# A TensorE gate step in fp32r halves, with GpSimd making the low half, and exponentials placed behind the gate steps

## What is computed

```python
def peer_ffn(h, peer_wq, peer_k1, peer_k2, peer_u, peer_v):      # 512 tokens, 8 heads, 128 x 128 keys
    s1, s2 = ...                                     # scores of each head's two query halves with 128 keys
    v1, i1 = lax.top_k(s1, 16)
    v2, i2 = lax.top_k(s2, 16)
    cand = (v1[..., :, None] + v2[..., None, :]).reshape(T, PEER_HEADS, 256)
    sc, pos = lax.top_k(cand, 16)
    e1 = jnp.take_along_axis(i1, pos // 16, axis=-1)
    e2 = jnp.take_along_axis(i2, pos % 16, axis=-1)
    experts = e1 * 128 + e2                                      # 8 x 16 = 128 experts a token
    gates = jax.nn.softmax(sc, axis=-1)
    ...
    a = gelu(einsum("ckd,cd->ck", peer_u[experts], h)) * gates
    return einsum("ck,ckd->cd", a, peer_v[experts])
```

## Time and profile before

| | |
|---|---|
| median of 3 runs | 2980.7 us (2978.4 to 2987.61) |
| the profiled execution | 2978.2 us |
| its span | 2976.5 us |
| TensorE busy | 2824.8 us, 95% |
| VectorE busy | 2235.7 us, 75% |
| ScalarE busy | 1481.7 us, 50% |
| GpSimd busy | 582.0 us, 20% |
| up stage | about 1784 to 2428 us |
| down stage | from 2431 us |

### The profile page before, as it was taken

One profiled execution on the slowest core, in us unless ns is written; L12 is line 12 of the kernel. 1 busy time (PEld: TensorE's weight loads), 2 busy tenths in 40 slices (PEclk: granted clock), 3 DMA queues, 4 the chain that ended last, 5 costly groups with the idle time before them and its releaser, 6 DMA issues.

```text
span 2976.5 us, 37320 instructions
## 1 busy us (share of the span) xinstructions
PE 2824.8 (95%) x13639; PEld 2359.7 (79%) x13639; DVE 2235.7 (75%) x3019; ACT 1481.7 (50%) x1990; POOL 582.0 (20%) x460
## 2 busy tenths in 40 slices
PE   5989987999999989999999999899999999999998
PEld 3666756888888857776777789899999998888887
DVE  6465546888888863696964599999777658888886
ACT  3433235888888843544552333555665633333332
POOL 0200111111111100000000000233333324444442
PEclk7999998999999999999999999999999999999999
DMA  7544635999999833232334324688998999999995
GB/s 305 171 160 146 212 137 205 368 372 367 363 360 352 324 140 128 86 114 89 117 106 149 114 86 142 236 293 308 322 319 310 326 337 358 368 364 357 362 371 174
DMA packets 201771, 737.90 MB, mean 248 GB/s; under 512 B 24432, under 2 KB 77808, under 8 KB 145008
## 3 DMA queue, kind: packets, MB, share of 16 engines
q1 hardware_dynamic: 124656, 497.12, 46.3%
q0 software_dynamic: 55056, 170.87, 16.7%
q10 hardware_dynamic: 21872, 67.48, 5.9%
HBM read 666.61 MB, written 93.91 MB: 256 GB/s over the span
## 4 chain that ended last, share of the span: by engine, by line
PE 64%; DVE 13%; issue 4%; ACT 2%; DMA 1%; ACTq 0%; DVEq 0%; SPq 0%; POOLq 0%
PE PS L544 55%; DVE wlo L1891 3%; PE PS L1145 2%; PE PS L1011 1%; PE PS L1023 1%; DVE hf L2700 1%; ACT whi L1221 1%; PE PS L850 1%; DVE oh L2674 1%; DVE hf L2688 1%; ACT HH L1861 1%; DVE cand L2640 1%; DVE cand L2642 1%; PE PS L1002 1%; DVE sS L2727 0%
## 5 line engine op out<-in xcount | busy, mean ns | idle before, releaser
L1891 DVE TENSOR_TENSOR wlo<-raw,whi 128x2048 fp32r<-128x2048 f32 x392 | 894.2, 2289 | 311.9 <-ACT whi L1221 270.9
L1221 ACT ACTIVATE whi<-raw 128x2048 fp32r<-128x2048 f32 x392 | 750.7, 1916 | 371.5 <-PE PS L544 317.3
L544 PE MATMUL PS<-HH,whi 128*128 128x512 f32 (+1 forms) x2056 | 787.8, 383 | 20.1 <-ACT HH L1257 10.1
L544 PE MATMUL PS<-HH,wlo 128*128 128x512 f32 (+1 forms) x2056 | 750.6, 365 | 0.0
L544 PE MATMUL PS<-HL,whi 128*128 128x512 f32 (+1 forms) x2056 | 750.3, 365 | 0.0
L544 PEld LDWEIGHTS PS<-HH,whi 128*128 128x128 f32 x2056 | 390.5, 190 | 78.1 <-issue 20.4
L544 PEld LDWEIGHTS PS<-HL,whi 128*128 128x128 f32 x2056 | 390.6, 190 | 46.6 <-issue 7.7
L544 PEld LDWEIGHTS PS<-HH,wlo 128*128 128x128 f32 x2056 | 389.3, 189 | 43.3
L544 PE MATMUL PS<-whi,HH 128*128 128x512 f32 (+1 forms) x896 | 350.6, 391 | 11.1 <-DVE HL L2730 5.8
L544 PE MATMUL PS<-whi,HL 128*128 128x512 f32 (+1 forms) x896 | 346.8, 387 | 0.0
L544 PE MATMUL PS<-wlo,HH 128*128 128x512 f32 (+1 forms) x896 | 346.8, 387 | 0.0
(11 more groups left out here) (434 smaller groups left out, 3891.9 us busy)
## 6 DMA issues: line engine op xcount, KB each, us to landing
raw<-in_moe_dram SPq DMA_DIRECT2D x192, 1024.0 KB, 7.2
raw<-in_u_units_dram SPq DMA_DIRECT2D x64, 1024.0 KB
raw<-in_v_units_dram SPq DMA_DIRECT2D x64, 1024.0 KB
raw<-in_w_in_dram SPq DMA_DIRECT2D x44, 1024.0 KB
raw<-in_w_ada_dram SPq DMA_DIRECT2D x24, 1024.0 KB, 20.1
acts_dram<-sS ACTq DMA_DIRECT2D x64, 384.0 KB
gates_dram<-XT ACTq DMA_DIRECT2D x24, 1024.0 KB
sS<-acts_dram SPq DMA_DIRECT2D x42, 384.0 KB
```

What stands on the lines that cost most here:

```text
L544: ins = t.matmul(dst, a, b, start=(first and n == 0), stop=(last and n == 2))
L1221: a.inc(a.e.activation(m.whi[p % HRING][:, :, :], m.raw[RAW_SLOT[load_of(p)]][:, :, :], ACT.Copy), "hi", p)
L1891: v.inc(v.e.tensor_tensor(m.wlo[h][:, :, :], m.raw[RAW_SLOT[load_of(p)]][:, :, :], m.whi[h][:, :, :].bitcast(F32), ALU.subtract), "lo_v", p)
```

## The change

Four edits go together. (1) The weighted one-hot is rounded to fp32r and a second, low one-hot is made of the weight's rest; TensorE multiplies both by the second one-hot matrix in fp32r, 8 matmuls instead of 4 in fp32. (2) The rest of the weights, `glow`, comes from one subtraction of VectorE per choice; GpSimd multiplies the one-hots by it, 128x512 per step, into the columns of the first 128 tokens in `HH` and `HL`, which the dense stage does not use (`gate_low`). GpSimd works on n = s-3 and ScalarE's weighting moves to n = s-4, since it overwrites the one-hots that GpSimd reads. (3) The exponential of a choice stands three units behind its last step, and behind that unit's gate step on ScalarE; VectorE's share stands a unit later. A choice has nine steps, and its gates may start only a unit after the share. (4) The planner counts 650 ns for a gate step instead of 1100.

```diff
-CHOICE_NS = (1500, 4600, 4600, 2000, 3400, 3400, 3400, 3400, 800, 700)
+CHOICE_NS = (1500, 4600, 4600, 2000, 3400, 3400, 3400, 3400, 800)
+EXP_AFTER, SHARE_AFTER, SHARE_NS = 3, 4, 700
...
-        row = ([], [], [])
+        row = ([], [], [], [i for i in chosen if n == chosen[i] + EXP_AFTER], [i for i in shared if n == shared[i]])
...
-        first = chosen.get(TD // 128, n)
+        vector += SHARE_NS * len(row[4])
+        first = shared.get(TD // 128, n)
         while (b * (LAST_GATE - first) < GATE_STEPS * (n - first) and b < GATE_STEPS and len(row[1]) < 2
-               and (b >= N_GATE or n > chosen.get(TD // 128 + b // 32, n))):
+               and (b >= N_GATE or n > shared.get(TD // 128 + b // 32, n))):
             row[1].append(b)
             b += 1
-            tensor += 1100
+            tensor += 650
...
+def gate_low(m, n):
+
+    return (m.HH, m.HL)[n % 4 // 2][:, 4 * (n % 2):4 * (n % 2) + 4, 0:TD]
...
         for k in range(4):
-            ins = t.matmul(m.PS[:, 5 + n % 3, 128 * k:128 * k + 128], m.oh[:, n % 4, 0, k, :],
-                           m.oh[:, n % 4, 1, k, :], start=True, stop=True)
+            out = m.PS[:, 5 + n % 3, 128 * k:128 * k + 128]
+            t.matmul(out, m.oh[:, n % 4, 0, k, :], m.oh[:, n % 4, 1, k, :], start=True, stop=False)
+            ins = t.matmul(out, gate_low(m, n)[:, k, :], m.oh[:, n % 4, 1, k, :], start=False, stop=True)
...
-    n = step - 3
+    n = step - 4
     if 0 <= n < N_GATE:
         k, q = divmod(n, 32)
-        a.wait_ge("onehot", n)
-        a.wait_ge("eT", TD // 128 + k)
+        a.wait_ge("lowered", n)
+        a.wait_ge("eT_part", TD // 128 + k)
...
-        for step in PEER[n][0]:
-            act_choice_step(a, m, step)
         for step in PEER[n][1]:
             act_gate_step(a, m, step)
+        for i in PEER[n][3]:
+            act_choice_exp(a, m, i)
...
+        if q == 0:
+            if k > 1:
+                v.wait_ge("lowered", 32 * (k - 1) - 1)
+            v.inc(v.e.tensor_tensor(m.glow[:, k % 2, :], m.PS[:, 4, 256:384], eT[:, 256:384], ALU.subtract), "glow",
+                  TD // 128 + k)
...
         for step in PEER[n][1]:
             dve_gate_step(v, m, step)
+        for i in PEER[n][4]:
+            dve_choice_share(v, m, i)
...
+def pool_gate_step(g, m, step):
+
+    n = step - 3
+    if 0 <= n < N_GATE:
+        k, q = divmod(n, 32)
+        g.wait_ge("glow", TD // 128 + k)
+        g.wait_ge("onehot", n)
+        g.inc(g.e.tensor_tensor(gate_low(m, n), m.oh[:, n % 4, 0, :, :].bitcast(F32),
+                                bass.AP(m.glow, 128 * (k % 2) + 4 * q, [[256, 128], [1, 4], [0, 128]]), ALU.mult),
+              "lowered", n)
...
     for n in range(128):
+        for step in PEER[n][1]:
+            pool_gate_step(g, m, step)
         for step in PEER[n][2]:
```

More of the change, by code:

```diff
@@ L194, in peer_schedule @@
             i, r = choice_of(a)
-            if r == 0 and a and n == chosen[choice_of(a - 1)[0]]:
-                break
             row[0].append(a)
@@ L200, in peer_schedule @@
             if r == CHOICE_STEPS - 1:
-                chosen[i] = n
+                chosen[i], shared[i] = n, n + SHARE_AFTER
         up.append(row)
@@ L222 @@
     "peer_a": "xrow sq5 root5",
-    "choice": "top pick gsub gt index onehot",
+    "choice": "top pick gsub gt index glow onehot",
     "conv_a": "mean csq cdev zaff zact fstep",
@@ L516, in __init__ @@
                 self.eT = [sb(s2, "eT", [128, 384]), self.rstd]
-                self.oh = sb(s2, "oh", [128, 4, 2, 4, 128])
+                self.glow = sb(s2, "glow", [128, 2, 128])
+                self.oh = sb(s2, "oh", [128, 4, 2, 4, 128], F32R)
             with ExitStack() as s2:
@@ L1133, in pe_gate_step @@
         else:
-            pe.wait_ge("eT", i - 1)
+            pe.wait_ge("glow", i - 1)
         for k, src in enumerate((m.e1, m.e2, m.gt)):
@@ L1778, in act_scores, with act_choice_exp @@
     a.mark("scored")
[L1781 to L1786, removed]
+def act_choice_exp(a, m, i):
+    a.wait_ge("gsub", i)
+    dst = m.act0[:, :] if i * 128 < TD else m.gt[:, i, :, :].rearrange("p h k -> p (h k)")
+    a.inc(a.e.activation(dst, dst, ACT.Exp), "gexp5", i)
 def act_gate_step(a, m, step):
@@ L1810, in act_gate_step @@
             a.wait_ge("onehot", 32 * (k - 1) - 1)
-        a.inc(s.activation(m.eT[k % 2][:, 0:384], m.PS[:, 4, 0:384], ACT.Copy), "eT", i)
-    n = step - 3
+        a.inc(s.activation(m.eT[k % 2][:, 256:384].bitcast(F32R), m.PS[:, 4, 256:384], ACT.Copy), "eT_part", i)
+        a.inc(s.activation(m.eT[k % 2][:, 0:256], m.PS[:, 4, 0:256], ACT.Copy), "eT", i)
+    n = step - 4
     if 0 <= n < N_GATE:
         k, q = divmod(n, 32)
-        a.wait_ge("onehot", n)
-        a.wait_ge("eT", TD // 128 + k)
+        a.wait_ge("lowered", n)
+        a.wait_ge("eT_part", TD // 128 + k)
         for j in range(4):
             t = 256 + 4 * q + j
-            a.inc(s.activation(m.oh[:, n % 4, 0, j, :], m.oh[:, n % 4, 0, j, :], ACT.Copy,
+            a.inc(s.activation(m.oh[:, n % 4, 0, j, :], m.oh[:, n % 4, 0, j, :].bitcast(F32), ACT.Copy,
                                scale=m.eT[k % 2][:, t:t + 1]), "weighted_part" if j < 3 else "weighted", n)
@@ L2654, in dve_choice_step, with dve_choice_share @@
                               ALU.subtract), "gsub", i)
[L2655 to L2661, removed]
+def dve_choice_share(v, m, i):
+    e = v.e
+    dst = m.act0[:, :] if i * 128 < TD else m.gt[:, i, :, :].rearrange("p h k -> p (h k)")
+    G3 = dst.rearrange("p (h k) -> p h k", h=8)
+    v.wait_ge("gexp5", i)
+    v.inc(e.tensor_reduce(m.gs[:, :], G3, AX.X, ALU.add), "pick")
+    v.own()
+    v.inc(e.reciprocal(m.gs[:, :], m.gs[:, :]), "pick")
+    v.own()
+    v.inc(e.tensor_tensor(G3, G3, bass.AP(m.some, 16, [[32, 128], [1, 8], [0, 16]]), ALU.mult), "gt", i)
 def dve_gate_step(v, m, step):
```

2 lines of the change are left out of this document (1 added, 1 removed).

## The result

The changed kernel takes **2995.52 us** (median of 5 runs, 2991.67 to 2998.93), against 2983.20 (2978.4 to 2987.61, 5 runs) for the kernel before in the same comparison: a ratio of 1.0041, with a 95% interval from 1.003 to 1.0051. It is slower, by about 12 us. The profiled execution has a span of 2989.9 us, 13.4 more than before.

The account below looks back on a forecast made before the run. TensorE was taken as the bound, with VectorE the late engine in the up stage; losses of 25 + 5 + 1 = 31 against 24 today give +7, so 2980.7 + 7 = 2988. Range 2957 to 3003; central case 2980 to 2998, chance 0.48.

Parts of the forecast that it names:

- Gate matmuls: On TensorE, a gate's 8 fp32r matmuls would cost 0.89 us, no change, ends 0.85 to 0.93.
- The exponentials: On ScalarE, standing three units later, they would by themselves remove TensorE's three long stops, up to 23 us.
- GpSimd's product: New 128x512 multiply on GpSimd, 96 times: about 1.0 us each, ends 0.95 and 1.89.
- VectorE to unit 72: Up stage: VectorE ends unit 72 at 2129 without contention, at 2172 with 43 us of it added.
- The chain behind a one-hot: Between VectorE's one-hots and the gate in unit 75, GpSimd and ScalarE need 2.3 us.
- TensorE's stops: Up stage: 25 us in many gaps, 5 of refill and clock losses, 1 at unit 17; 31 against 24 lost.
- The first small stop: On TensorE at unit 17, transposes behind the share: a stop of 1 us stays.
- Behind unit 72 no more stops: Late up stage: VectorE needs 9.1 us with GpSimd of 10.1 per two units, so it catches up.
- No contention: Up stage: VectorE loses nothing to speak of to GpSimd, lost 24 us shrink to 1 to 3: 2959; chance 0.23.
- Dearer product: Each GpSimd product takes 1.3 us from VectorE: +20, 3001; from 1.5 us late to the stage's end; chance 0.17.
- Cheaper matmuls: On TensorE a gate costs 0.5 to 0.65 us: 2930 without contention, 2974 with it; chance 0.07.
- Exponentials that do nothing: Moving them gains nothing, since VectorE's lateness reaches TensorE through the one-hots anyway: 2978 to 2983; chance 0.05.

Follow-up runs that it names:

- the memset: The changed kernel with GpSimd writing zeros by memset instead of its product, the gate's low half left out of the result: 2968.92 us, 0.9959.
- the doubled one: The changed kernel with GpSimd's product made twice in a row, same operands and result: 3057.04 us, 1.0249.
- the placing alone: The kernel before plus nine-step choice, later exponentials and shares, planner's 650; gates in fp32, no GpSimd product: 2963.94 us, 0.9938.

## Why the prediction came out as it did

Forecast 2988 from a sum of +7; measured +12, inside the 2980 to 2998 given for this case. The mechanism was the predicted one: VectorE loses time to GpSimd's products, up to unit 72, and TensorE stops for it. That the sum came so near is in part luck, since errors in its terms cancel. Point by point:

**Gate matmuls**, 0.89 us each and no change: measured 0.907, +1.3 us, within the 0.85 to 0.93. The rows of the same form decided it; the halved gate that the prediction weighs against them did not come.

**The exponentials.** Said to take the three long stops away, up to 23 us alone. They did: ScalarE's four exponentials (starts 1848.02, 1903.93, 2042.60, 2186.69) have no idle time in front, where the earlier trace rows showed 11.13, 8.19 and 8.77. Alone, and with the plan, they gave 17 us of the 23; the waits for the first rows stood behind them. With the rows later too, the kernel with fp32 gates is 23 to 24 us faster.

**GpSimd's product**, "about 1.0 us": 1.03 to 1.05 alone.

**VectorE to unit 72.** This was the term on which the sum rests: choice 3's gsub near 2172. It began at 2176.93, the one of choice 0 at 1891.87 (predicted 1889): 285 us, against 240 of work + 43 of contention = 283. Adding up what every instruction of this stretch takes over its mean of before gives 37 us beside 49 products, 0.76 each and not 0.86 (32 of it on the weight halves, one-hots, dot products and L2648, of which 40 of 141 are longer at all). Waits of VectorE are 8 us, of which 4.9 are for rows, and the sum had none. The remaining 240 is the work, as predicted. With memsets the same stretch takes 251 us, 34 less. The share of contention that is hidden was an estimate, a seventh; it was about a quarter.

**The chain behind a one-hot.** The prediction allowed 2.3 us for GpSimd and ScalarE between a one-hot and its gate. The shortest in the trace is 3.4 us. At all seven gate stops the one-hot had been finished 0.9 to 4.6 us before its product began, and GpSimd had a row gather in front; in five of the seven it was 3.43 us, and in four of these the gather waited for a dot product of VectorE (which frees its buffer). At the stop of 1.46 us at 1968.52 (one-hot ready at 1961.45):

```profile
1963.38 1.47 POOL L3054 DMA_INDIRECT ht<-in_peer_u_dram,IDX  x1 [1.03 <-DVE dots L2705]
...
1964.88 2.22 POOL L3040 TENSOR_TENSOR HL<-oh,glow 128x512 fp32r<-128x512 f32 x1
```

From the one-hot's end to the gate this is 7.1 us. The prediction had gathers waiting behind a product; products waiting behind a gather it left out. So a late VectorE reaches TensorE through the gathers as well. How much of the 12 us that adds was not isolated.

**TensorE's stops**, 25 in gaps of 1 to 5 us, 1 at unit 17 and 5 behind them: the stops sum to 18.7, and with the clock and refill behind them the stage lost 34.3 us beyond its work of units, gates and transposes, where 31 was said (24.2 before). So the sum was right within 3 us because two errors cancel: stops of 18.7 and not 26, and losses behind them of 15.6 and not 5. The granted clock (third from the end of each row) tells of a part of these losses. It fell at four of the thirteen stops and not at others:

```profile
2060.30:2068.50 8.20, 8.20 (x42) 8.20 (x42) 8.11 (x7) 5.25 (x16) 6.79 (x5) 0.71 0.84 311
2195.00:2200.00 5.00, 5.00 (x34) 5.00 (x33) 4.86 (x7) 4.24 (x8) 3.10 (x3) 1.00 0.99 365
```

The first is unit 53, behind the stop of 4.25 us; the second follows the stop of 1.44 at 2194.17. The place was right: the largest stop in unit 52, by choice 2's share, and units 52 and 53 took 12.57 and 8.16 us. The first small stop, put at 1 us in unit 17, did not come; one of 0.18 stands at the start of unit 16, behind a weight half. "Behind unit 72 no more stops" was a little off: the one of 1.44 us stands in unit 77, and then none.

**What was missed** is the first rows, whose gathers hold up GpSimd's product (the stops in units 26 and 27) and VectorE (3.68 us). Rows for it stood in the trace of before, a wait of 1.16 us on VectorE at 1900.25, in the shadow of the stop of 9.11; I asked what a removed stall makes late next, but only of the engines, not of the transfer that flew in its cover. It is of the size of the 5 us between +7 and +12: moving the rows two units away is worth 4 us without the halves and 5 with them, though the second of these runs has a new stop of 10 us in it, so that the share of this wait in the 12 us isn't told apart from that of the losses behind short stops.

**The rivals.** No contention: refuted by the trace and by the memset, which removes it and gives 2969. Dearer product: refuted as a price (0.76, not 1.3 us); that the cost runs to the end of the stage beyond some point is confirmed by the doubled one, at 1.3 us a gate and not only from 1.5. Cheaper matmuls: refuted by the gate's starts. Exponentials that do nothing: refuted by the placing alone.

## What to carry to other kernels

Before work is handed to an idle engine, add up what it takes from the one that is short: a GpSimd product of 1.04 us that reads SBUF cost VectorE 0.7 us on average here, and what that did to the end went by VectorE's slack (27 us for the first 96, 62 for the next). Price a matmul by a row of its own form, not by its type. When a stall is removed, look for the transfers that were in flight during it: they were the next wait here. Look at what stands in front of new work in the queue that gets it, too. And where two edits are bundled, time them apart: here one was worth 17 us and the other cost 34.

## What the runs showed of the hardware

- The exclusion goes both ways and by whole instructions: at 2068.29 the product waits for the end of a one-hot, and the dot product issued at 2069.20 for the end of the product. One-hots lost at most 0.84 us with single products; with two in a row the median lost 0.83 and only one of 96 more than that (2.378 in all). The longest losses stand where an instruction of VectorE begins during a row gather that a product follows: two dot products lost 1.62 us each (2.84 in all), the cast above 1.55.
- A memset of GpSimd of the same size (0.53 us), which writes SBUF and reads nothing, cost the one-hots (1.214 to 1.228 us), weight halves and dot products beside it nothing. Four short instructions with one input were held up by 0.34 to 0.50 us, once, between 1944.86 and 1946.25, around a row gather and a memset.
- VectorE's custom dot product, with two inputs, is held up like a tensor_tensor (2.06 us at 2069.20), and so were a few casts and tensor_scalars with one input; its reduction of 1024 columns with one input stays at 1.220 us.
- At 128 moving columns a matmul in fp32r starts 0.11 us after the last, as does each record of an fp32 one: 8 fp32r matmuls took 0.84 us, 4 in fp32 0.81.
